# Feed-forward norms applied per token after the gate and up products, plain transposes of x begun inside the output projection, expert blocks of 96 tokens, and two table fills issued at other places

## The reference

```python
def rms_norm(x, g):
    xf = x.astype(F32)
    y = xf * lax.rsqrt(jnp.mean(xf * xf, axis=-1, keepdims=True) + RMS_EPS)
    return (y * g.astype(F32)).astype(x.dtype)
...
    return merged.astype(x.dtype) @ w_out
...
def swiglu(x, w_gate, w_up, w_down):
    return (jax.nn.silu(x @ w_gate) * (x @ w_up)) @ w_down
...
        x = x + hybrid_mixer(
...
        h = rms_norm(x, norm_ffn[layer])
        i = layer // 2
        if layer % 2 == 0:
            x = x + swiglu(h, w_dense_gate[i], w_dense_up[i], w_dense_down[i])
        else:
            x = x + moe_ffn(h, w_router[i], w_moe_gate[i], w_moe_up[i], w_moe_down[i])
```

## Time and profile before

| | |
|---|---|
| three runs | 1451.08, 1453.42, 1453.69 us (median 1453.42) |
| the profiled execution | 1450.7 us, span 1448.9 us |
| mean granted TensorE clock | 0.984 |
| TensorE busy | 1378.4 us, 95% |
| VectorE busy | 1154.0 us, 80% |
| ScalarE busy | 867.1 us, 60% |
| POOL busy | 49.7 us, 3% |
| moved | 394 MB, 272 GB/s over the span |

### The profile page before, as it was taken

One profiled execution on the slowest core, in us unless ns is written; L12 is line 12 of the kernel. 1 busy time (PEld: TensorE's weight loads), 2 busy tenths in 40 slices (PEclk: granted clock), 3 DMA queues, 4 the chain that ended last, 5 costly groups with the idle time before them and its releaser, 6 DMA issues.

```text
span 1448.9 us, 19057 instructions
## 1 busy us (share of the span) xinstructions
PE 1378.4 (95%) x6518; PEld 1122.9 (78%) x6518; DVE 1154.0 (80%) x1169; ACT 867.1 (60%) x918; POOL 49.7 (3%) x62
## 2 busy tenths in 40 slices
PE   6999988999998999897999999999999999999994
PEld 3887677788887876676888887888878888888884
DVE  5979875545439898855988989889898898888985
ACT  4345644443425445533777777777777777777873
POOL 0020011000000110101000000000000000000001
PEclk9999999999999999998999999999999999999997
DMA  8444134975443344133998989989899899998993
GB/s 291 165 180 162 59 119 154 384 294 191 152 174 117 145 145 175 65 132 117 404 378 331 418 306 422 405 312 415 331 400 405 311 422 358 362 403 313 422 400 142
DMA packets 62625, 394.09 MB, mean 272 GB/s; under 512 B 7154, under 2 KB 7726, under 8 KB 22650
## 3 DMA queue, kind: packets, MB, share of 16 engines
q1 hardware_dynamic: 58506, 377.74, 67.0%
q10 hardware_dynamic: 2208, 8.91, 1.6%
q0 software_dynamic: 1872, 6.92, 1.4%
HBM read 376.76 MB, written 16.78 MB: 272 GB/s over the span
## 4 chain that ended last, share of the span: by engine, by line
issue 53%; PE 38%; DVE 6%; ACT 1%; DMA 1%; POOL 1%; SPq 0%; ACTq 0%; POOLq 0%; DVEq 0%
PE bank L1280 9%; PE bank L1281 9%; PE bank L1327 5%; PE bank L1535 4%; PE bank L1512 2%; PE bank L1322 2%; PE bank L1293 2%; PE bank L1417 1%; DVE ys L862 1%; PE bank L1430 1%; PE bank L1410 1%; DVE tmp L862 1%; DVE stat L1086 1%; DMA got<-slot_y,rowi 0%; ACT x_squared L622 0%
## 5 line engine op out<-in xcount | busy, mean ns | idle before, releaser
L873 DVE TENSOR_TENSOR w_lo<-raw,w_hi 128x2048 fp32r<-128x2048 f32 (+2 forms) x382 | 802.6, 2109 | 133.1 <-ACT w_hi L596 123.9
L596 ACT ACTIVATE w_hi<-raw 128x2048 fp32r<-128x2048 f32 (+2 forms) x382 | 673.8, 1769 | 157.4 <-PE bank L1535 74.8
L1280 PE MATMUL bank<-w_hi,hT_hi 128*128 128x512 f32 (+1 forms) x1232 | 489.9, 398 | 5.6 <-DVE act L1182 1.7
L1281 PE MATMUL bank<-w_hi,hT_lo 128*128 128x512 f32 (+1 forms) x1232 | 477.9, 388 | 0.0
L1280 PEld LDWEIGHTS bank<-w_hi,hT_hi 128*128 128x128 f32 x1232 | 232.4, 189 | 54.9 <-issue 7.1
L1281 PEld LDWEIGHTS bank<-w_hi,hT_lo 128*128 128x128 f32 x1232 | 232.5, 189 | 43.6 <-issue 1.0
L1512 PE MATMUL bank<-w_lo,hT_hi 128*128 128x512 f32 (+1 forms) x880 | 231.9, 386 | 0.0
L1512 PEld LDWEIGHTS bank<-w_lo,hT_hi 128*128 128x128 f32 x880 | 163.7, 188 | 33.8 <-DVE w_lo L873 2.7
L1535 PE MATMUL bank<-w_hi,act_hi 128*128 128x512 f32 (+1 forms) x440 | 119.3, 393 | 0.8 <-ACT act_hi L783 0.8
L1535 PE MATMUL bank<-w_hi,act_lo 128*128 128x512 f32 (+1 forms) x440 | 118.6, 392 | 0.0
L1535 PE MATMUL bank<-w_lo,act_hi 128*128 128x512 f32 (+1 forms) x440 | 117.7, 390 | 0.0
(11 more groups left out here) (190 smaller groups left out, 943.7 us busy)
## 6 DMA issues: line engine op xcount, KB each, us to landing
raw<-in_moe SPq DMA_DIRECT2D x224, 1024.0 KB, 7.3
raw<-in_mix SPq DMA_DIRECT2D x56, 1024.0 KB, 4.9
raw<-in_dense SPq DMA_DIRECT2D x28, 1024.0 KB, 4.9
raw<-in_moe SPq DMA_DIRECT2D x42, 512.0 KB, 3.5
raw<-in_moe SPq DMA_DIRECT2D x16, 768.0 KB, 7.3
slot_h<-x_squared ACTq DMA_DIRECT2D x1, 6656.0 KB, 44.7
slot_y<-y SPq DMA_DIRECT2D x9, 512.0 KB, 8.6
tok<-slot_h SPq DMA_DIRECT2D x8, 512.0 KB, 8.0
```

Source lines behind the costliest of these rows:

```text
L596: nc.scalar.activation(HI[:, split_slot, 0:width], RAW[:, raw_slot, 0:width], ACT.Copy)\
L873: vec.tensor_tensor(LO[:, split_slot, 0:width], RAW[:, raw_slot, 0:width], HI[:, split_slot, 0:width].bitcast(F32), ALU.subtract).then_inc ...
L1280: mm(out_, left[0], right[0], start=start, stop=False)
L1281: mm(out_, left[1], right[1], start=False, stop=False)
```

## The change

- **Norm.** `fht` is a plain transpose of x (`turn_h`), with no diagonal matrices. In layer 0 the per-token factor 1/rms enters as the scale of the SiLU and in VectorE's product (`scalar_tensor_tensor` with `STAT[:, 4 + tb]`). In layer 1 the ranking of the logits does not need it, the difference of the two best is multiplied by it, and the rows sent to the experts carry it as before.
- **Place.** Transposes of column blocks 0 to 3 (x after `wo0`) stand between the two slabs of `wo1`; those of blocks 4 to 7 stand behind the first gate slab (layer 0) or behind the first half of the router products (layer 1). The copies and remainders on ScalarE and VectorE move with them, and VectorE splits the first two feed-forward slabs before it adds the second half to x.
- **Blocks.** `CAP` is 96, so `XTRA` is 5. An expert may have two extra blocks; the bookkeeping has some more small steps. Operations on a block's tokens have 96 rows or columns.
- **Fills.** Both tables have 1536 rows and are filled whole; `slot_h` ahead of ScalarE's loop over the chunks of the dense block, `slot_y` behind it.

```diff
-CAP = P
+CAP = 96
 XTRA = (T * TOPK) // (CAP + 1)
 NBLK = NE + XTRA
-SLOT_ROWS = (NBLK + 2) * CAP
+SLOT_ROWS = -(-(NBLK + 2) * CAP // P) * P
...
-        tt(tv[:, 2, :], tv[:, 1, :], tv[:, 0, :], ALU.subtract, sem("top_diff"), 1)
+        tt(tv[:, 2, :], tv[:, 1, :], tv[:, 0, :], ALU.subtract)
+        v.settle()
+        tt(tv[:, 2, :], tv[:, 2, :], STAT[:, 4:4 + TB], ALU.mult, sem("top_diff"), 1)
...
+        tt(R["end"][:, :], cnt[:, :], over[:, :], ALU.add)
+        v.settle()
         for j in range(XTRA):
-            stt(oh[:, j, :], cnt[:, :], float(j), over[:, :], ALU.is_equal, ALU.mult)
+            ts(R["within"][:, j, :], R["end"][:, :], float(j), None, ALU.is_gt)
+        v.settle()
+        for j in range(XTRA):
+            stt(oh[:, j, :], cnt[:, :], float(j), R["within"][:, j, :], ALU.is_le, ALU.mult)
...
+            turned_h(0)
+            turned_h(1)
+            split_to(first, stage)
+            for half in range(2):
+                for tb in range(TB):
+                    wait_drained(act, layer, f"wo{half}", tb)
+                    squares(2 * tb + half, "norm_ffn")
+                if half == 0:
+                    split_to(first + 1, stage)
+                elif layer == 0:
+                    split_to(first + 2, stage)
+            turned_h(2)
+            turned_h(3)
...
-                    ins = nc.scalar.activation(R["silu"][:, tb, 0:width], src, ACT.Silu)
+                    src = PS[tb if layer == 0 else parity][0:rows, 0:width]
+                    scale = STAT[:, 4 + tb:5 + tb] if layer == 0 else 1.0
+                    ins = nc.scalar.activation(R["silu"][0:rows, tb, 0:width], src, ACT.Silu, scale=scale)
...
+                if not is_moe:
+                    act.wait_ge(sem("zeros_ready"), 1)
+                    clear(slot_h)
                 with act.Fori(0, 4) as i:
...
+                if not is_moe:
+                    clear(slot_y)
                 turned_hi(qb + NCH - 2)
...
+                    if step == "wo1":
+                        turned_h(0)
+                        turned_h(1)
...
+                        split_to(FIRST["ffn", layer] + 1, ("ffn", layer))
...
-            diagonal("norm_ffn", "hf_ready")
...
+                    if layer == 0:
+                        ins = vec.scalar_tensor_tensor(out=to, in0=up, scalar=STAT[:, 4 + tb:5 + tb], in1=silu,
+                                                       op0=ALU.mult, op1=ALU.mult)
...
+        def turn_h(layer, i):
+
+            for tb in range(TB):
+                wait_drained(pe, layer, f"wo{i // 2}", tb)
+            bank_free(layer, "fht", i)
+            for j in range(4):
+                kd, tb = 2 * i + j // 2, j % 2
+                ins = turn(bank("fht", i)[:, j * P:(j + 1) * P], X[:, tb, kd * P:(kd + 1) * P])
+            fill(layer, "fht", i, ins)
...
+                            if step == "wo1" and part == 0:
+                                turn_h(layer, 0)
+                                turn_h(layer, 1)
...
+                    if kd == 4:
+                        turn_h(1, 2)
+                        turn_h(1, 3)
...
+                    if part == 0 and not is_moe:
+                        turn_h(0, 2)
+                        turn_h(0, 3)
```

More of the change, by code:

```diff
@@ L726, in _, with turned_h @@
                              event(f"{step}_hi", layer), i + 1)
-            if layer == 1:
-                act.wait_ge(sem("moe_loaded"), 48)
-                copy(R["wr_parts"][:, :, 0, :], R["wr"][:, :, :], sem("wr_hi_ready"), 1)
             stage = ("ffn", layer)
             first = FIRST[stage]
-            for half in range(2):
-                for tb in range(TB):
-                    wait_drained(act, layer, f"wo{half}", tb)
-                    squares(2 * tb + half, "norm_ffn")
-                split_to(first + half * (2 - layer), stage)
-            for i in range(4):
+            def turned_h(i):
                 wait_filled(act, layer, "fht", i)
@@ L767, in ffn_split @@
                       (first + p) % SPLIT_SLOTS, width)
-            tbs = TB if layer == 0 else 1
+            tbs, rows = (TB, P) if layer == 0 else (1, CAP)
             def silu(q, n, parity, width=CHUNK):
@@ L928, in _, with turned_h @@
             fb, fpm = R["fb"], R["fpm"]
+            def turned_h(i):
+                dve.wait_ge(event("fht_hi", layer), 2 * i + 2)
+                for j in range(2):
+                    kd = 2 * i + j
+                    stt(HTL[:, kd, :], bank("fht", i)[:, j * T:(j + 1) * T], PAR[:, PAR_GF + kd:PAR_GF + kd + 1],
+                        HTH[:, kd, :].bitcast(F32), ALU.mult, ALU.subtract,
+                        *(drain_of(layer, "fht", i) if j else (None, None)))
             def norm_rope(step, c, rstd_at):
@@ L1396, in _ @@
                     wait_drained(pe, layer, "av3", 0)
-                elif step == "fht":
-                    pe.wait_ge(event("hf_ready", layer), TB)
                 for i in range(len(banks)):
```

84 lines of the change are left out of this document (42 added, 42 removed).

## The result

The changed kernel takes 1436.77 us (median of 4 runs, 1433.2 to 1438.62); the kernel before, beside it, 1452.72 us (4 runs, 1451.08 to 1453.69). The ratio is 0.989, 95% interval 0.9877 to 0.9904. The forecast was 1437.

What follows compares the result with a forecast made beforehand. TensorE was taken as the limit, full in the dense and expert blocks, so gains count at hand-overs or in its own stream. Terms sum to -16.3 us, 1450.7 to 1434.4; with 2.7 for the median 1437 us, range 1430 to 1443.

Steps and rivals of the forecast that it cites:

- Term A: First hand-over, layer 0: norm leaves the waiting string and transposes start early, -8.5 us; three-operand product in first chunk, +0.1.
- the clock at 1.00 through it: Sign of being right: full granted clock from layer 0's projection to gate slab 4, without a TensorE gap over 0.5 us.
- Term B: Second hand-over, layer 1: the last router products end at 663.7 instead of 669.4 us, -5.7 us.
- Gathers, -1.2: The 16 gathers before the first expert block move 96 columns for 128, between 0 and -1.6 us, taken as -1.2.
- Bookkeeping, +1.0: First expert block: eight more small VectorE operations at 0.1 to 0.2 us, on the path, +1.0 us.
- Blocks, -1.6: Eight expert blocks: only transposes and last copies shrink with 96 tokens, 0 to 0.7 us a block, taken as 0.2.
- Fills, 0: Table fills around layer 0's dense loop: moving them counts nothing, up to 3 us a fill as the bound.
- rival (b): A fill lands late for layer 1 or its issue holds ScalarE: 1441 to 1443 us, chance 0.09.
- (a): Fewer stationary columns shorten every product of an expert block, 11 us: 1426 us, chance 0.10.
- (c): Something else, above all VectorE, is late at the hand-overs and the gain halves: 1444 us, chance 0.10.
- (d): An expert with 97 to 128 tokens needs a ninth block, priced 93.3 us: 1530 us, chance 0.03.
- (e): The transposes wait all the same, so no change within 0.2%: 1453 us, chance 0.02.

Runs made afterwards that it cites:

- late: Changed kernel with all 16 transposes behind the output projection and ScalarE's and VectorE's steps in the old order: 1446.72 us, ratio 0.9961 to the kernel before.
- again2: Changed kernel unedited, run once more beside a later set: 1438.13 us, ratio 0.9903 to the kernel before.
- rest_early: Changed kernel with the router's remaining bookkeeping issued ahead of the low part of the first gathered block: 1434.58 us, ratio 0.9885 to the kernel before.
- again: Changed kernel unedited, run as the control for the other experiments, with a second trace: 1436.97 us, ratio 0.9903 to the kernel before.
- cap128: Changed kernel with blocks of 128 tokens instead of 96: 1440.01 us, ratio 0.9911 to the kernel before.
- warm: Changed kernel with products that nobody reads put in TensorE's waits: 1433.44 us, ratio 0.9877 to the kernel before.
- b_fills: Kernel before with only its two fills moved to where the change has them: 1451.62 us, ratio 1.0001 to the kernel before.
- warm_rest: Changed kernel with both unread products in TensorE's waits and the router's remaining bookkeeping issued earlier: 1432.78 us, ratio 0.9875 to the kernel before.

## Why the prediction was right, and where it was wrong

- **Term A, -8.5 + 0.1.** Measured -8.53, and the timeline shows the steps: no gap before gate slab 4, transposes 0.79 us, the wait for the first chunk's product a little longer. late gives 6.6 of it to the place and 1.9 to the norm; the walk by rows gave the sum right.
- **No term for the clock in the dense block.** The forecast costed the wait for chunk 0's product at its length alone (+0.1). That wait was there before too, 1.73 us, with the clock at 1.00 behind it; now, at 1.93 us, the clock sometimes falls behind it: +1.6 us in the profiles of after, again2 and rest_early, nothing in again and cap128. It is a term between 0 and 1.6. The sign named for it, "the clock at 1.00 through it", covered only the stretch to slab 4, and there it held.
- **Term B, -5.7.** Measured -4.2. The prediction calls S the end of the projection's first half, but 5.44 us before the projection's end is the end of `wo1`'s first slab, where the transposes stand (644.23 in after); the first half itself ended 10.9 us before the projection. Taken from there, the walk's times to S + 9.1 hold; the step that failed is "the last 16 router products" at 0.112 each. They came 0.213 apart at the half clock, after a wait of 1.40 us: 16 x 0.1 = 1.6 us, the whole difference. rest_early, where the clock stayed up, and warm both show them at 0.11.
- **Gathers, -1.2.** Measured +0.55 (6.32 to 6.87). The step that failed is "it goes with the clock and thus mostly with the columns". It goes with the clock and not with the moving columns: 96 and 128 of them both take 6.8 us at the half clock, and 3.8 at the full one (warm's gathers with 96, L1430 with 128). What is left to pace one such product, 0.215 us here, is its load of 128 weight columns; that is inferred, and it does not extend to transposes, whose 8 of a block load 128 weight columns too and come 0.084 us apart with 96 moving columns and 0.099 with 128, both at the full clock (fences of cap128). The Trainium skill ("TensorE: Matmul & The Clock Gate", LDWEIGHTS) gives P / 1.2 ns for a load of P columns, an estimate of 107 ns for these, as one figure; the router products agree at the full clock (0.111), but they measure twice that at the half (0.213), and the transposes lie under it, so the measurement decides. Of before, 6.32 had its last part at the full clock.
- **Bookkeeping, +1.0.** Measured +0.7 from the first expert product to the first load; rest_early shows that it is this and that 1.2 us come back.
- **Blocks, -1.6.** Measured -2.3 (0.33 a pitch, 0.32 by cap128), inside 0 to 0.7 a block: a term of the right kind taken too low. What was wrong in it is the premise that the transposes are bounded by their load as the router products are: they come faster than those, and their time fell with the moving columns, by 0.4 us a block.
- **Fills, 0.** Right as a difference, and shown by b_fills. The second fill landed 18.5 us after its issue at 390.1, at 408.6, for the squares at 429.04, so the estimate by 412 held and rival (b) is out. The next slabs were fetched from 405.4 only, as the prediction had read from before. But the reason given, some 3 us in hand, hid how much the move matters: left in place the fills would cost 11.4 us. The Trainium skill ("DMA: Bandwidth & Descriptors", Queues, rings and completion order) says that a DMA engine takes turns between the queues that have work. From that the prediction took at least half of the engines for the fill, and that did not come out where slab fetches ran beside a fill all the time. From 252 to 292 us in after, slot_h's fill had 38% of the engines' time and moved 6.3 of 16.3 MB. By the profile it moved 1549 packets of 4.1 KB there, and the slabs' queue 1195 of 7.3 KB; how the turns are made no run here shows.
- **The total.** Against the forecast the profiled pair lacks 4.2 us of gain. The medians do not lack them, because that pair stands apart by chance: before 2.0 us under its median and after 1.8 over. In again, where one of the clock's falls is absent, the span is 14.6 us under before's, and 1.7 us are missing. So 1437 is right with a sum whose parts are right to 1.6 us, all three misses towards less gain and all three in stretches at the half clock; part of the agreement is luck. The later sets say the same: again was 15.1 us under the before beside it and again2 13.0, where the sum said 16.3.
- **Rivals.** (a) is out by the pitches of after and cap128, (b) as said above. (c) asked for half of the hand-over gain to go; 12.7 of 14.1 us stayed. (d) and (e) did not occur.

## What to carry to other kernels

Work that needs only part of a result can be begun inside the product that makes the rest, and the gain is then more than the wait removed, where TensorE comes out of it at its full clock (layer 0: 3.8 us of waiting and 2.4 of half clock). Cost every short wait twice: once for its length, and once for what runs at half the clock behind it, above all instructions of few columns, which took twice as long at the half clock whatever their moving columns; a few products that nobody reads, put in the wait, kept the clock here and made the runs alike. A fill or store of many megabytes should be issued where the engine that issues the next one has nothing due: a second transfer of 2 to 6 MB behind one of 6.3 MB on the same queue held ScalarE for 12.6 to 13.3 us.

## What the runs showed of the hardware

- After TensorE's waits of 1.4 to 1.9 us the clock falls in some executions and not in others with the same timeline (after and again at chunk 0; again and rest_early before the late router products). I found nothing in these traces that tells beforehand which. With the waits filled down to 0.3 to 1.1 us it fell at neither place in the profiled runs of warm and warm_rest.
- A product with 128 weight columns and few moving ones takes 0.11 to 0.12 us at the full clock and 0.21 at the half, with 8, 16, 96 or 128 moving columns; that its load sets it is inferred from this. Transposes differ: with 128 weight columns they come 0.099 us apart with 128 moving columns and 0.084 with 96, at the full clock. Loads of 96 columns take 161 ns by the records against 188 for 128, and under 512 moving columns the difference does not show (cap128).
- The issue of a fill on ScalarE's queue took 0.4 to 0.7 us with up to 8 groups of 128 rows of 4 KB (4.2 MB) ahead of it and 12 in all. Behind 12 groups (6.3 MB) it took 12.6 to 13.3 us, whether it asked for 4, 8 or 12 itself, and behind 13 in the kernel before 5.9 us.
- A fill with slab fetches beside it all the time had 38% of the DMA engines' time (after, 252 to 292 us: 6.3 of 16.3 MB), not half; its packets had 4.1 KB, those of the slabs 7.3.
